# Two-layer hybrid decoder trunk on one core: layer 0's input handed over turned, its norm applied behind the products

## What is computed

```python
def rms_norm(x, g):
    y = xf * lax.rsqrt(jnp.mean(xf * xf, axis=-1, keepdims=True) + NORM_EPS)
    return (y * g.astype(jnp.float32)).astype(x.dtype)
...
    z = hn @ w_in                        # layer 0: 1024 x 3584
    u, v, g_a, q, k, vv, g_b = jnp.split(z, cuts, axis=-1)
    y_a = chunked_gmlp(u, v, ln_g, ln_b, w_s, b_s) * jax.nn.silu(g_a)
    y_b = moba_attention(...)            # causal attention of 8 heads at this length
    y_b = y_b * jax.nn.silu(g_b)
    return jnp.concatenate([y_a, y_b], axis=-1) @ w_out
...
    z = hn @ w_in                        # layer 1: 1024 x 4096
    q, k, v, g = jnp.split(z, [C_WIDTH, 2 * C_WIDTH, 3 * C_WIDTH], axis=-1)
    y = dilated_mixture(...)             # 16 heads
    return (y * jax.nn.silu(g)) @ w_out
```

## Time and profile before

| | us |
|---|---|
| runs | 278.44, 278.5, 280.25 |
| median of the runs | 278.5 |
| profiled execution, its own time | 279.57 |
| its span (first to last instruction) | 277.8 |
| around the span | 1.77 |
| PE, DVE, ACT, POOL busy | 266.2, 182.2, 162.1, 16.6 |

### The profile page before, as it was taken

One profiled execution on the slowest core, in us unless ns is written; L12 is line 12 of the kernel. 1 busy time (PEld: TensorE's weight loads), 2 busy tenths in 40 slices (PEclk: granted clock), 3 DMA queues, 4 the chain that ended last, 5 costly groups with the idle time before them and its releaser, 6 DMA issues.

```text
span 277.8 us, 4330 instructions
## 1 busy us (share of the span) xinstructions
PE 266.2 (96%) x1637; PEld 237.2 (85%) x1637; DVE 182.2 (66%) x341; ACT 162.1 (58%) x316; POOL 16.6 (6%) x38
## 2 busy tenths in 40 slices
PE   6979999999999999999999999999999999999990
PEld 6858999888888888888788999999999888888880
DVE  2886759895879397576777527494953958542643
ACT  3947685778484365256547637478676875650132
POOL 4140000100110000001100000000000001000021
PEclk9989999999999999999999999999999999999997
DMA  6986992654306634454554970828043323100004
GB/s 216 381 222 216 378 352 90 210 173 151 151 2 223 230 106 135 149 173 145 182 170 139 349 274 3 268 60 278 5 152 149 114 96 107 66 0 0 2 0 151
DMA packets 22499, 43.53 MB, mean 157 GB/s; under 512 B 1344, under 2 KB 1872, under 8 KB 22480
## 3 DMA queue, kind: packets, MB, share of 16 engines
q1 hardware_dynamic: 22336, 42.74, 46.0%
q0 software_dynamic: 144, 0.52, 0.6%
HBM read 42.22 MB, written 1.05 MB: 156 GB/s over the span
## 4 chain that ended last, share of the span: by engine, by line
PE 88%; DVE 5%; ACT 4%; POOL 1%; issue 1%; POOLq 0%; DVEq 0%
PE products L896 16%; PE products L898 16%; PE products L897 16%; PE products L886 7%; PE products L884 7%; PE products L882 7%; PE turned L821 4%; DVE k_low L702 2%; PE attended L837 2%; PE attended L940 2%; PE attended L939 2%; PE scores L916 2%; PE scores L915 2%; DVE w_lo L670 2%; PE attended L938 2%; PE attended L821 1%
## 5 line engine op out<-in xcount | busy, mean ns | idle before, releaser
L670 DVE TENSOR_TENSOR w_lo<-w_raw,w_hi 128x1024 fp32r<-128x1024 f32 x76 | 91.0, 1222 | 10.7 <-ACT w_hi L529 9.9
L529 ACT CAST w_hi<-w_raw 128x1024 fp32r<-128x1024 f32 x76 | 78.1, 1049 | 34.1 <-PE products L898 15.6
L896 PE MATMUL products<-w_hi,hnT_hi 128*128 128x512 f32 x144 | 58.4, 406 | 0.6 <-DVE w_lo L670 0.6
L897 PE MATMUL products<-w_hi,hnT_lo 128*128 128x512 f32 x144 | 56.9, 395 | 0.0
L898 PE MATMUL products<-w_lo,hnT_hi 128*128 128x512 f32 x144 | 56.9, 395 | 0.0
L882 PE MATMUL products<-hnT_hi,w_hi 128*128 128x256 f32 x192 | 54.6, 285 | 0.0
L886 PE MATMUL products<-hnT_hi,w_lo 128*128 128x256 f32 x192 | 54.3, 283 | 0.0
L884 PE MATMUL products<-hnT_lo,w_hi 128*128 128x256 f32 x192 | 54.3, 283 | 0.0
L884 PEld LDWEIGHTS products<-hnT_lo,w_hi 128*128 128x128 f32 x192 | 36.8, 192 | 0.1
L882 PEld LDWEIGHTS products<-hnT_hi,w_hi 128*128 128x128 f32 x192 | 36.7, 191 | 0.1
L886 PEld LDWEIGHTS products<-hnT_hi,w_lo 128*128 128x128 f32 x192 | 36.7, 191 | 0.0
(11 more groups left out here) (124 smaller groups left out, 340.3 us busy)
## 6 DMA issues: line engine op xcount, KB each, us to landing
w_raw<-in_c_w_in SPq DMA_DIRECT2D x16, 1024.0 KB, 5.5
w_raw<-in_ab_w_in SPq DMA_DIRECT2D x12, 1024.0 KB, 5.6
w_raw<-in_ab_w_out SPq DMA_DIRECT2D x4, 1024.0 KB, 5.0
w_raw<-in_c_w_out SPq DMA_DIRECT2D x4, 1024.0 KB, 5.1
w_raw<-in_ab_w_in SPq DMA_DIRECT2D x4, 512.0 KB, 6.6
h<-in_x SPq DMA_DIRECT2D x2, 512.0 KB, 5.5
out<-hn SPq DMA_DIRECT2D x4, 256.0 KB, 2.2
gate<-in_final_norm_g POOLq DMA_DIRECT2D x1, 512.0 KB, 4.3
```

Source lines behind the costliest of these rows:

```text
L529: nc.scalar.copy(w_hi[:, n % SPLIT_SLOTS, :, :], w_raw[:, half % RAW_SLOTS, part, :]).then_inc(hi_ready, 1)
L670: nc.vector.tensor_tensor(w_lo[:, n % SPLIT_SLOTS, :, :], w_raw[:, half % RAW_SLOTS, part, :], w_hi[:, n % SPLIT_SLOTS, :, :].bitcast(fp32 ...
L896: nc.tensor.matmul(to[:], xh, w_hi[:, slot, half_item, :], start=begins, stop=False)
L897: nc.tensor.matmul(to[:], xl, w_hi[:, slot, half_item, :], start=False, stop=False)
```

## The change

The host hands over x turned (channels on the partitions) with the gains in front, the spatial weights turned and the bias laid out by position. The kernel rounds and subtracts `x * gain` straight from that, with no norm, and no turns. The value group becomes one group over both tiles like the others, so layer 0 has one group number less. Its first quarter is split chunk by chunk, and x's chunks are interleaved with the quarters. 1/rms is found meanwhile from the untransposed x and applied behind the products: as a per-position scale for values, gates and GELU; and for queries and keys, whose positions lie along the free dimension, by a full tile of 1/rms (`rstd_rows`, made by two matmuls) with which DVE multiplies each bank into `tanh`, before ACT's copies and DVE's subtractions, which now read `tanh`. Warm-up is 12 products of a tile of ones.

```diff
+    out = []
+    for quarter in range(4):
+        if quarter:
+            out += [("turned_x", 2 * quarter), ("turned_x", 2 * quarter + 1), ("round", quarter), ("rest", quarter)]
+        else:
+            out += [("turned_x", 0), ("first_round", 0), ("first_rest", 0), ("turned_x", 1), ("first_round", 1),
+                    ("first_rest", 1)]
...
-    at(HIDDEN_1_AT, ("hidden", 1))
-    at(2 * first_item[2] + WINDOWS_AT, ("windows", 0))
-    even = 2 * first_item[4]
-    at(even + WS_AT, ("ws", 0))
+    at(2 * first_item[1] + ROWS_AT, ("rows", 0))
+    at(2 * first_item[1] + WINDOWS_AT, ("windows", 0))
+    even = 2 * first_item[3]
...
+            for n, (matrix, chunk, column) in enumerate(HALVES):
...
+                if n == 0:
+
+                    sp.dma_start(w_raw[:, 0, 0], rows[:, 0]).then_inc(w_first[0], 16)
+                    sp.dma_start(w_raw[:, 0, 1], rows[:, 1]).then_inc(w_first[1], 16)
+                    sp.dma_start(w_raw[:, 0, 2:4], rows[:, 2:4]).then_inc(w_loaded[0], 16)
+                    continue
...
+                if n == 2:
+                    for t in range(TILES):
+                        sp.dma_start(h[:, t, :], x_tiles[t]).then_inc(x_loaded[t], 16)
+                if n == 3:
+
+                    sp.dma_start(wsT, gmlp_w_s[0]).then_inc(ws_loaded, 16)
...
         @block.scalar
         def _(act):
+            nc.scalar.dma_start(first_x, x_turned[:, 0:2 * CHUNKS + SEQ]).then_inc(xT_loaded[0], 16)
+            nc.scalar.dma_start(xT[:, 1:2], rest_of_x[:, 1:2]).then_inc(xT_loaded[1], 16)
+            nc.scalar.dma_start(xT[:, 2:4], rest_of_x[:, 2:4]).then_inc(xT_loaded[2], 16)
+            nc.scalar.dma_start(xT[:, 4:8], rest_of_x[:, 4:8]).then_inc(xT_loaded[3], 16)
...
+                if what == "turned_x":
+                    act.wait_ge(xT_loaded[0], 16)
+                    act.wait_ge(xT_loaded[(0, 1, 2, 2, 3, 3, 3, 3)[n]], 16)
+                    nc.scalar.mul(hnT_hi[:, n, :], xT[:, n, :] if n else xT_0,
+                                  first_gain[:, n:n + 1]).then_inc(xT_hi, 1)
...
-                        for i, bank in enumerate(pair(n)):
+                        for i, bank in enumerate(split_source(n)):
+                            if set_of_heads(n) == 0:
+                                act.wait_ge(heads_scaled, 2 * count_of_kind(SPLIT_KINDS, n - 1) + i + 1)
                             for side in range(2):
...
                             last.then_inc(heads_high, 1)
+                            if kind == "key" and KEYS_AGAIN_BY[i] == "act":
+                                keys_again(act, nc.scalar.copy, n, i)
...
+                    if heads_set == 0:
+
+
+                        dve.wait_ge(products_done, LAST_ITEM_OF_GROUP[n] + 1)
+                        dve.wait_ge(rows_ready, 1)
+                        if banks_before:
+                            dve.wait_ge(heads_high, banks_before)
+                            dve.wait_ge(heads_low, banks_before)
+                        for i, bank in enumerate(pair(n)):
+                            nc.vector.tensor_tensor(
+                                tanh[:, i, :].rearrange("p (a b) -> p a b", b=SEQ),
+                                bank[:].rearrange("p (a b) -> p a b", b=SEQ),
+                                rstd_rows[:].unsqueeze(1).to_broadcast([P, 2, SEQ]), ALU.mult).then_inc(heads_scaled, 1)
...
+            pe.wait_ge(ones_ready, 1)
+            for _ in range(WARM):
+                nc.tensor.matmul(value_bank[:, 0:P], ones[:], ones[:], start=True, stop=True)
...
+                    if kind == "value":
+                        pe.wait_ge(xT_lo, chunk + 1)
+                        if n == 0 and half_item == 1:
+                            pe.wait_ge(lo_ready, 1)
```

More of the change, by code:

```diff
@@ L107, in plan @@
     u, v, ga, q, k, vv, gb = (i * BLOCK for i in range(7))
-    groups.extend([("value_half", 0), ("value_half", 1)])
-    halves.extend(("even_in", part * HALF_CHUNKS, vv) for part in range(2))
-    for tile in range(TILES):
-        items.extend((tile, i, q_, 0) for i in range(2) for q_ in range(2))
+    whole("even_in", vv, "value", 0)
     whole("even_in", q, "query", 0)
@@ L189, in steps @@
     for n, item in enumerate(ITEMS):
-        turns = min(turns + (RATE if item[3] is None else RATE / 2), MOST_TURNS)
+        if n >= 2:
+            turns = min(turns + (RATE if item[3] is None else RATE / 2), MOST_TURNS)
         for half in range(2):
-            while half == 0 and n >= 4 and split < 2 * len(HALVES):
+            while half == 0 and n >= 2 and split < 2 * len(HALVES):
                 soon = first_use[split] <= n + SOON
@@ L198, in steps @@
                     break
+                if split == 6:
+                    out.append(("squares", 0))
                 out.append(("round", split))
@@ L541, in _ @@
                             last.then_inc(heads_high, 1)
-                    elif kind == "value_half":
-                        nc.scalar.mul(v[:, place, 0:BLOCK], pair(n)[0][:], 0.5).then_inc(act_emptied, 1)
+                            if kind == "key" and KEYS_AGAIN_BY[i] == "act":
+                                keys_again(act, nc.scalar.copy, n, i)
+                    elif kind == "value":
+                        act.wait_ge(rstd_parts, 2)
+                        for t, bank in enumerate(pair(n)):
+                            last = nc.scalar.mul(v[:, t, 0:BLOCK], bank[:], rstd[:, t:t + 1])
+                        last.then_inc(act_emptied, 1)
                     elif kind == "value_tile":
@@ L854, in _ @@
                     if half_item == 0:
-                        if kind == "value_half":
-                            pe.wait_ge(hidden_ready, 2 * place + (chunk0 > 0) + 1)
-                        pe.wait_ge(lo_ready, 2 * half + quarter + 1)
+                        if n:
+                            pe.wait_ge(lo_ready, 2 * half + quarter + 1)
                         if group >= 2 and group not in started:
@@ L892, in _ @@
                             targets = [(place, pair(group)[side])]
+                        if n == 0 and half_item == 0:
+                            pe.wait_ge(first_hi, 1)
+                            for wait, x_part, w_part in ((None, hi, w_hi), (None, lo, w_hi), (first_lo, hi, w_lo)):
+                                if wait is not None:
+                                    pe.wait_ge(wait, 1)
+                                for t, to in targets:
+                                    nc.tensor.matmul(to[:], x_part[:, 0, t * P:(t + 1) * P], w_part[:, 0, 0, :],
+                                                     start=wait is None and x_part is hi, stop=False)
+                            continue
                         for t, to in targets:
@@ L966, in _ @@
                     last.then_inc(y_turned, 1)
[L967 to L971 removed]
+                elif what == "rows":
+                    pe.wait_ge(const_pool, 2)
+                    pe.wait_ge(rstd_parts, 2)
+                    for t in range(TILES):
+                        last = nc.tensor.matmul(turn_bank[:, t * P:(t + 1) * P],
+                                                rstd[:, t:t + 1].to_broadcast([P, P]), ident[:], start=True, stop=True)
+                    last.then_inc(rows_turned, 1)
                 elif what == "hidden":
[L973 removed]
+                    if n == 0:
                         pe.wait_ge(mixed, TILES)
                     hidden_turn(n)
[L976 to L981 removed]
+_NAMES = ("x", "x_turned", "final_norm_g", "ab_w_in", "ab_w_out", "gmlp_ln_g", "gmlp_ln_b", "gmlp_w_s",
+          "gmlp_b_s", "c_w_in", "c_w_out")
 def kernel(**inputs):
```

269 lines of the change are left out of this document (138 added, 131 removed).

## The result

| | before | changed |
|---|---|---|
| runs (lowest to highest, number) | 278.44 to 280.43 (8) | 280.85 to 282.25 (8) |
| median, us | 278.69 | 281.56 |
| ratio, 95% interval | 1 | 1.0087, 1.0061 to 1.0114 |
| profiled execution, own time | 279.57 | 281.70 |
| its span | 277.8 | 279.7 |

275.5 us was forecast, and 281.6 lies outside the range of 269.0 to 279.5.

The account below looks back on a forecast made before the run. PE, busy 266.2 of 277.8 us, was taken to bound the kernel. Scores 4.6 us earlier, less 1.6 for the low clock, gave 3.0 us: median from 278.5 to 275.5 us, range 269.0 to 279.5.

Parts of the forecast that it names:

- Behind this point: From layer 0's first turn on: all lists as before, so the 3.0 us gained by then reach the kernel's end.
- The value group: Layer 0's start: 48 products from 6.9 us end at 18.0 instead of 27.44, a head start of 9.4 us.
- The seventh half: Weight load needed for rounding quarters 12 and 13: lands at 29.6 us, behind 10.23 MB; bounds 28.0 and 32.1.
- The DVE queue: DVE's in-order work from quarter 13's last rest at 32.8 to the keys at 46.6: 13.8 us.
- (a): Layer 0, first scores to first turn: PE would wait 1.3 us for the first head's exponentials, done 6.5 behind the scores.
- (b): Behind PE's wait at layer 0's first scores: the clock falls to its lower level, costing 1.6 us, at most 2.5.
- The edits put at nothing: Per-position scales, GpSimd's small steps, 1/rms rows and bank reuse: covered by distance, cost nothing.
- Loads at full rate: Rival at the start: two queues load at full rate, half seven lands at 28.0, time 273.9 us; chance 0.20.
- The whole head start: Rival in layer 0: DVE reaches the keys by about 42, all is kept, time 269.1 us; chance 0.12.
- Slow loads: Rival at the seventh half: loads hold 298 GB/s, it lands at 34.3, time 280.2 us; chance 0.07.
- The low clock in the value group: Rival at the start: PE starves between first quarters, 48 products end at 27.5, time 279.0 us; chance 0.06.
- What I had not seen: Anywhere in the kernel: remaining chance for causes not listed, 0.03, one third of it slower.

Follow-up runs that it names:

- e4: The changed kernel with 22 products of ones by ones ahead of layer 0's first scores, where PE waits: 280.41 us, ratio 1.0042.
- e6: The changed kernel with masks early, small tensors late, and layer 1's key copies as in the kernel before: 274.61 us, ratio 0.9835.
- e2: The kernel before with only ACT's second copy of the keys' first bank moved between the banks' copies, in all three places: 281.3 us, ratio 1.0073.
- e8: The changed kernel without the 1/rms scaling of layer 0's queries and keys (output not the reference's): 277.84 us, ratio 0.9964.
- e9: e6 with only the first two heads' scores, first turn and third head's scores one half item later: 274.47 us, ratio 0.985.
- e5: The changed kernel with the small tensors (0.79 MB) loaded behind the eighth half instead of the fourth: 278.39 us, ratio 0.9975.
- e3: The changed kernel with layer 1's masks on DVE moved from half item 18 to half item 8: 277.6 us, ratio 0.9924.
- e7: e6 with the first five heads' steps two half items or fewer later in the list: 278.69 us, ratio 0.9972.

## Why the prediction was wrong, step by step

**The step that failed** is the sentence "Behind this point every list is as before, PE has no hole to speak of, and the end ... is untouched: nothing grows or shrinks." The diff showed the extra pair of copies inside the loop over the banks, with no condition on the layer beside it, and I had looked at the order of ACT's list at layer 0 only. The prediction's own sign of being wrong, a new wait of PE beyond layer 0's first heads, is what came. In layer 1 the keys' evacuation decides when the first heads are ready, as it did before; 1.2 us of copies were pushed in front of half of it. By the profiled executions the forecast was 276.6 and the result 281.70, 5.1 us apart: 1.9 of them are this step, 2.9 are layer 0 (first turn 0.1 instead of 3.0 earlier), 0.2 lie around the span.

In layer 0 the same copies were put down as lying beside DVE's subtractions. That holds for the first bank's; but DVE waits 1.09 us for the second bank's copies there too (53.02), and the first head's probabilities come later by up to that. In the changed kernel the slow products hide it. With the clock at full PE waits about as long at the first turn (1.11 us in e4, 1.08 in e6), and e2 shows 0.3 us. No run took the copies out of layer 0 alone in the changed kernel, so what they cost there stays open.

**The rest is the sum of small terms, nearly all of one sign**, each a later arrival than was put down. The mechanism (head start, late half, DVE's queue, wait ended by `k_low`, low clock behind it) is in every row where it was said to be.

| step | predicted | measured |
|---|---|---|
| value group ends | 18.0 | 18.77 |
| seventh half rounded from | 29.6 | 30.85 |
| rest of quarter 13 ends | 32.8 | 34.29 |
| DVE turns to the keys | 46.6 | 48.44 |
| PE's wait at the scores | 4.4 | 5.58 |
| first scores | 50.0 | 52.08 |
| scores to first turn | 6.8 | 7.7 |
| first turn, against before | -3.0 | -0.1 |

- *The value group*: one wait of 1.15 us for a `w_lo` at 10.43 where I had allowed a few tenths.
- *The seventh half* is the largest: 1.25 us. It has two terms of opposite sign. The stretches of the changed kernel:

```profile
0.00:14.00 14.00, 11.80 (x51) 10.29 (x52) 7.77 (x13) 8.96 (x15) 2.53 (x14) 1.00 0.90 322
14.00:28.00 14.00, 14.00 (x100) 13.18 (x99) 6.64 (x7) 9.35 (x12) 4.67 (x8) 1.00 1.05 387
29.00:30.00 1.00, 1.00 (x11) 1.00 (x10) 0.66 (x1) 1.00 (x2) 0.00 (x0) 1.00 0.06 25
```

  The first 14 us moved 322 GB/s and not 298, so 9.9 MB had come by 28 us, and nearly all of the 10.23 that I had added up was through before 29 (355 GB/s in the mean to 28.75). What I had wrong is that the half lands when the bytes are through: ACT begins to round it at 30.85. From 29 to 30 us the DMA share is 0.06 at 25 GB/s, which is one of the 16 engines at its full pace (394 over 16 is 24.6) with the other fifteen idle. The whole half waits for the pieces of that one. Why one engine lies behind stays open.
- *The DVE queue*: from the rest of quarter 13 to the keys 13.8 us were put down, and it is 14.15. The multiplications, for which I had 0.7 each between 0.28 and 1.2, take 0.64. The hole of 1.84 us, in which DVE waits for ACT behind the late eighth half, is wider than the 1.3 worked out (ACT 1.5 behind, its two copies 1.2, less the two multiplications, 1.4).
- *Behind the scores*: of (a) and (b) the larger was to count. It does: PE has no hole from the scores to the turn, and the clock alone sets the 7.7 us. Only the size was off: 7.7 less before's 5.2 is 2.5 us for (b), its upper bound, where I had taken 1.6 from a wait of 1.84 us. (a) is beneath it, as e4 shows: 6.4 measured, 6.5 worked out.
- *The edits put at nothing* cost nothing: no row shows a wait for the rows of 1/rms or for GpSimd's small steps, and the end of the kernel is as before.

**The rivals.** Loads at full rate: from 5 to 13 us the changed kernel, with two engines issuing loads, moved 395 GB/s, where the kernel before had 394 with one, so the second queue gave no rate. The prediction had cited the Trainium skill for that (DMA: Bandwidth & Descriptors, "Issuing engines are not separate DMA queues"); the trace agrees. The whole head start: it wasn't kept in any version, and e6 kept 5.2 of 8.7 us. Slow loads: the half is rounded from 30.85, and 32.6, the point from which that rival decides, was not reached. The low clock in the value group did not fall in the changed kernel's profile, but it did in e8's (0.67 from 10 to 14 us) and in e9's (0.57 from 12 to 16), in two of the ten profiles of kernels with this start: it is a hazard of single executions. What was right was not in my list: a second place in the program on which the moved copies act. What I had not seen had a chance of 0.03.

## What to carry to other kernels

When an edit sits in a helper or loop that several stages share, go through every stage that it serves and ask which of them stands on the path: here two of the five us of error came from a stage that the change was not about. A head start of one engine is worth only what the next engines' in-order lists and the loads let through, so follow them back instruction by instruction and expect each term to be late rather than early. Put a load down with the slowest of its pieces: here the half was used 2 us after nearly all of its bytes had come. And after such a change move the fillers (masks, small loads) out of the stretch in which the others now have to catch up: that, and the condition on the layer, turned a loss of 0.9% into a gain of 1.6% (274.6 us).

## What the runs showed of the hardware that I had not expected

- The wait before the clock falls can be short, and its length alone doesn't tell. At the first scores, with PE idle for 5.58 us the next four us had 0.50, with 2.41 (e5) the stretch from 50 to 54 had 0.60, with 1.81 (e3) 0.58, and with 1.37 (e6) 1.00. But in e3's value group a wait of 2.20 us (at 11.43) was followed by 1.00 (12 to 18 us), and so was one of 1.91 us in e7 (at 56.39; 1.00 from 56 to 60). What else counts in it stays open; no run here varied it apart.
- The low clock cost less than its duration: some five us at 0.50 (2.5 us of slower products) were worth 1.3 us in the rows (e4), because without them PE waits for ACT at the turn instead.
- The 16 DMA engines don't end a load together: between 29 and 30 us one of them alone was moving the seventh half (share 0.06, 25 GB/s), with the others at rest. Taking 0.79 MB from in front of that half brought its rounding forward by 2.2 to 2.4 us, of which the bytes are 2.0 at 387 GB/s.
